# Gate products of the recurrence's branch in 1024-column halves, four of eight pieces by seven block products

## What is computed

```python
h = rmsnorm(x, g_pre_mix[l])
proj = h @ w_in[l]
q_in, ckv, k_rope, lru_x, lru_y, gate_mla, gate_lru = jnp.split(proj, IN_SPLIT_IDX, axis=-1)
o_mla = mla_attention(q_in, ckv, k_rope, positions, g_ckv[l], w_ukv[l]) @ w_o_mla[l]
...
o_lru = (hr * jax.nn.gelu(lru_y, approximate=True)) @ w_o_lru[l]
merged = jax.nn.sigmoid(gate_mla) * o_mla + jax.nn.sigmoid(gate_lru) * o_lru
x = x + rmsnorm(merged @ w_out[l], g_post_mix[l])
```

## Time and profile before

| | us |
|---|---|
| median of 3 runs | 1725.56 |
| lowest and highest | 1725.15, 1725.76 |
| profiled execution | 1725.27 |
| its span | 1723.5 |
| PE busy in the span | 1714.5 (99%) |
| DVE busy | 1211.6 (70%) |
| ACT busy | 949.1 (55%) |
| POOL busy | 216.4 (13%) |
| bytes moved | 355.29 MB, 206 GB/s on average |

### The profile page before, as it was taken

How to read it: one execution, slowest core, us unless ns; L and a number is a source line. 1 busy time by engine, 2 the same in 40 slices (tenths; PEclk the granted TensorE clock), 3 DMA queues, 4 the chain that set the end, 5 groups by cost and what they waited for, 6 DMA issues and landing times.

```text
span 1723.5 us, 25132 instructions
## 1 busy us (share of the span) xinstructions
PE 1714.5 (99%) x8920; PEld 1461.9 (85%) x8920; DVE 1211.6 (70%) x1517; ACT 949.1 (55%) x1203; POOL 216.4 (13%) x271
## 2 busy tenths in 40 slices
PE   9999999999999999999999999999999999999998
PEld 8888888888888888888888888888888888888886
DVE  7766665467788874446567687778877778977766
ACT  7656655443667763334446575555545556545553
POOL 0012212110345431100000001110001110000000
PEclk9999999999999999999999999999999999999999
DMA  9644458997556579976655455556755556775552
GB/s 342 201 133 156 153 197 266 270 300 212 180 176 183 182 247 268 259 226 227 216 176 188 147 197 194 192 176 212 248 195 176 181 181 207 247 242 181 194 218 99
DMA packets 228384, 355.29 MB, mean 206 GB/s; under 512 B 7264, under 2 KB 163552, under 8 KB 224736
## 3 DMA queue, kind: packets, MB, share of 16 engines
q1 hardware_dynamic: 215232, 322.72, 55.6%
q0 software_dynamic: 7168, 16.78, 5.3%
q10 hardware_dynamic: 5920, 14.94, 2.3%
HBM read 350.22 MB, written 20.97 MB: 215 GB/s over the span
## 4 chain that ended last, share of the span: by engine, by line
PE 89%; issue 5%; ACT 2%; DVE 2%; POOL 0%; ACTq 0%; DVEq 0%; POOLq 0%
PE ps L554 43%; PE ps L617 34%; PE ps L1033 4%; PE ps L570 3%; ACT wsp L1162 1%; DVE wsp L1697 1%; PE ps L829 1%; PE ps L757 1%; PE ps L679 1%; PE ps L668 0%; ACT wsp L1613 0%; PE ps L649 0%; PE ps L786 0%; PE ps L762 0%; POOL scr L2575 0%
## 5 line engine op out<-in xcount | busy, mean ns | idle before, releaser
L1697 DVE TENSOR_TENSOR wsp<-raw,wsp 128x2048 fp32r<-128x2048 f32 (+2 forms) x303 | 673.3, 2236 | 262.4 <-ACT wsp L1162 249.8
L1162 ACT ACTIVATE wsp<-raw 128x2048 fp32r<-128x2048 f32 (+2 forms) x288 | 529.4, 1852 | 203.2 <-PE ps L617 170.9
L554 PE MATMUL ps<-asp,wsp 128*128 128x512 f32 x3064 | 542.4, 339 | 0.0
L554 PEld LDWEIGHTS ps<-asp,wsp 128*128 128x128 f32 x3064 | 469.7, 188 | 70.3 <-DVE asp L2158 0.3
L617 PE MATMUL ps<-wsp,hsp 128*128 128x512 f32 x1908 | 437.2, 390 | 0.0
L617 PEld LDWEIGHTS ps<-wsp,hsp 128*128 128x128 f32 x1908 | 357.9, 188 | 74.1
L554 PE MATMUL ps<-hsp,wsp 128*128 128x512 f32 (+1 forms) x1936 | 349.7, 340 | 0.0
L554 PEld LDWEIGHTS ps<-hsp,wsp 128*128 128x128 f32 x1936 | 297.5, 188 | 42.9
L617 PE MATMUL ps<-wsp,asp 128*128 128x512 f32 x768 | 175.6, 389 | 0.0
L1173 ACT ACTIVATE cr<-ps 128x256 f32<-128x256 f32 x185 | 69.3, 380 | 190.1 <-PE ps L554 173.6
L617 PEld LDWEIGHTS ps<-wsp,asp 128*128 128x128 f32 x768 | 144.0, 188 | 29.8
(11 more groups left out here) (293 smaller groups left out, 1249.6 us busy)
## 6 DMA issues: line engine op xcount, KB each, us to landing
raw<-in_w_up SPq DMA_DIRECT2D x88, 1024.0 KB, 5.3
raw<-in_w_in SPq DMA_DIRECT2D x64, 1024.0 KB, 5.5
raw<-in_w_down SPq DMA_DIRECT2D x28, 1024.0 KB, 4.9
raw<-in_w_in SPq DMA_DIRECT2D x32, 768.0 KB, 4.4
dn_sums<-in_w_down POOLq DMA_DIRECT2D x64, 256.0 KB, 6.9
raw<-in_w_o_mla SPq DMA_DIRECT2D x16, 1024.0 KB, 10.7
raw<-in_w_o_lru SPq DMA_DIRECT2D x16, 1024.0 KB, 7.5
raw<-in_w_out SPq DMA_DIRECT2D x16, 1024.0 KB, 4.9
```

What stands on the lines that cost most here:

```text
L554: mm = pe.matmul(ps[:, bank, 0:w], lhs(part, k), x[:, 0:w], start=(f and part == 0), stop=(l and n == 1))
L1162: act.activation(wsp[:, p0 % SLOTS, 0, 0:n], raw[:, p0 % SLOTS, 0:n], ACT.Copy).then_inc(hi_done, 1)
L1697: dve.tensor_tensor(wsp[:, slot, 1, 0:n], raw[:, slot, 0:n], wsp[:, slot, 0, 0:n].bitcast(F32), ALU.subtract).then_inc(lo_done, 1)
```

## The change

`PH_OL` becomes four phases: a gate phase and an output phase for columns 0 to 1023, then both for columns 1024 to 2047 (`PH_GL`, `PH_OL`, lists of two).

A gate phase has 12 pieces after `GL_PLAN`: pairs 0, 2, 4 and 6 of row blocks as plain pieces of 2 x 1024 (eight block products each), pairs 1, 3, 5 and 7 as a first and a made piece (seven block products). The plain products go to banks 4 to 7, the shared ones to banks 0 to 3. An output phase has 8 pieces of 2 x 1024, in banks 0 to 3.

```diff
+GL_PLAN = [("plain", 0), ("plain", 2), ("first", 1), ("made", 1), ("first", 3), ("made", 3),
+           ("plain", 4), ("first", 5), ("made", 5), ("first", 7), ("made", 7), ("plain", 6)]
...
-PH_OL = Phase(PH_LRU, 4, [0, 0, 0, 2] * 2, crosses=False)
-PH_WO = Phase(PH_OL, 4, [0] * 4)
+PH_GL, PH_OL = [], []
+for _half in range(2):
+    PH_GL.append(Phase(PH_OL[-1] if PH_OL else PH_LRU, 1, [0] * 12, twice=GL_FIRST))
+    PH_OL.append(Phase(PH_GL[-1], 1, [0] * 8))
+PH_WO = Phase(PH_OL[-1], 4, [0] * 4)
```

The work of DVE in the two phases (`sums_rest`, `first_low` as before in the down products, now with the phase as argument):

```diff
+            for h in range(2):
+                for c in range(LEAD, len(GL_PLAN) + LEAD):
+                    if c in GL_FIRST:
+                        sums_rest(PH_GL[h], c)
+                        first_low(PH_GL[h], c)
+                    else:
+                        lo(PH_GL[h], 0, c)
+                    if h == 0 and c == LEAD:
                         y_lo(PH_LRU.trips - 1)
+                    if h == 1 and c == LEAD:
+                        ol_merge(0)
+                    if c == GL_MADE[-1] + 2:
+                        gl_products(h)
+                for c in range(LEAD, 8 + LEAD):
+                    lo(PH_OL[h], 0, c)
+                    if c == 3:
+                        gl_plain(h)
+                    if h == 1 and c == 6:
                         merged_lo(range(8))
...
+            ol_merge(1)
```

```diff
-            for cs in DN_SUMS:
-                weight_sums(0, cs, sums_done)
+            for batch in SUM_BATCHES[:3]:
+                weight_sums(*batch)
...
-            for cs in DN_SUMS:
-                weight_sums(1, cs, sums_done)
+            for batch in SUM_BATCHES[3:]:
+                weight_sums(*batch)
```

More of the change, by code:

```diff
@@ L833, in _ @@
             rounds(pe, PH_LRU, lru, first_apart=True)
-            enter(PH_OL, [0, 1, 2, 3])
             def turn_merged(ks):
@@ L844, in turn_merged, with form_mm @@
                     turn(a_tok, k, 4 + k // 2 % 4, (k % 2) * T, m_turned)
-            def o_lru(i):
-                last = isinstance(i, int) and i == PH_OL.trips - 1
+            def form_mm(bank, lhs, slot, block, first, last):
+                for t, (part, low) in enumerate(TERMS):
+                    mm = pe.matmul(ps[:, bank, :], lhs(low), wsp[:, slot, part, quarter(block)],
+                                   start=(first and t == 0), stop=(last and t == 2))
+                return mm
@@ L1028, in _ @@
                     rounds(pe, up, up_round)
[L1031 to L1035, removed]
                 def dn_half(h):
@@ L1375, in merged_hi, with made_high @@
                     act.activation(hsp[:, k, 0:T], ps[:, 4 + k // 2 % 4, (k % 2) * T:(k % 2 + 1) * T], ACT.Copy).then_inc(m_hi, 1)
[L1377 to L1389 removed]
+            def made_high(ph, c, at):
+                slot = (ph.p0 + c) % SLOTS
+                act.wait_ge(gemm_step, free_step(ph, c))
+                act.wait_ge(landed[slot], ph.landed(0, c))
+                act.wait_ge(sums_made, at + 1)
+                act.activation(wsp[:, slot, 0, :], raw[:, slot, :], ACT.Copy).then_inc(hi_done, 1)
@@ L1390, in o_lru @@
                         merged_hi(range(8))
-                    if last and c == 6:
-                        merged_hi(range(8, 12))
-            rounds(act, PH_OL, o_lru, first_apart=True, last_apart=True)
+            for h in range(2):
+                gl_half(h)
+                ol_half(h)
             def mem_high(ks):
@@ L2027, in _, with sums_rest @@
-            rounds(dve, PH_OL, o_lru, first_apart=True, last_apart=True)
+            def sums_rest(ph, c):
+                first, made = (raw[:, (ph.p0 + at) % SLOTS, :] for at in (c, c + 1))
+                for at in (c, c + 1):
+                    dve.wait_ge(landed[(ph.p0 + at) % SLOTS], ph.landed(0, at))
+                own.link(dve.tensor_tensor(made[:, 1024:1536], made[:, 0:512], first[:, 1024:1536], ALU.add))
+                dve.tensor_tensor(made[:, 1536:2048], made[:, 1024:1536], first[:, 1536:2048], ALU.add).then_inc(sums_made, 1)
```

378 lines of the change are left out of this document (260 added, 118 removed).

## The result

The changed kernel is slower. Ten runs have a median of 1731.61 us (1726.20 to 1735.81); ten runs of the kernel before have 1725.82 us (1725.15 to 1727.59). The ratio is 1.0028, 95% interval 1.0018 to 1.0037. It is one of the longer ones: the ten runs spread over 9.6 us, and the three shortest (1726.20, 1726.52 and 1728.51 us) have a mean granted clock of 0.999, the other seven, from 1730.38 us on, 0.997 or 0.998.

A forecast was written before the change was run, and what follows sets the result against it. The prediction took the stage to be bound by PE alone, at its matmul rate. 1725.27 - 5.44 (matmuls removed) + 1.28 (waiting) = 1721.1; with the runs' median 0.29 above that execution, 1721.4 us, range 1720.0 to 1724.2.

The forecast's parts named there:

- The 24 matmuls: Gate, both halves: 12 fewer matmuls of 512 columns each, at 0.2267 us, saving 5.44 us.
- The start of the first half: First gate half, third to sixth piece: PE waits for DVE 1.28 us in all, 0.3 before the fourth piece.
- Rival B: First gate half's start: POOL's multiplication comes after DVE's three operations; 3.0 us of waiting, 1723.1 us; chance 0.16.
- The second gate half has no wait: Second gate half: DVE has a large lead at the first pair, so PE has no new wait.
- The sums of `h`, the gate's sums and `PH_WO`: Before, in and after the recurrence's branch: added or moved sums and output-bank order costed at nothing.
- The loads of the first gate half: First gate half, made pieces: loads land in 4.3 to 7.3 us, losing 0 to 1.0 us, taken as 0.
- rival C: Gate, first half: made pieces' loads land in 7 to 9 us; 1722.1 to 1724.1 us; chance 0.17.
- The new form has no dearer matmul: Gate pairs: a 512-column matmul costs 0.2267 us in the seven-product form, as in the plain one.
- changes between plain pieces: Gate, 40 pieces where there were 32: a change of piece costs PE nothing when the piece is ready.
- the banks of the products: Start of output phases: PE asks 5.44 us after the last made piece, four DVE operations take 2.8 us; costed at nothing.
- rival D: Gate, both halves: made pieces' loads land in up to 13.2 us, losing 11.3 us; 1731.4 us; chance 0.06.

The follow-up runs named there:

- e11: Changed kernel with 3 of POOL's 16 sums between the output phases' load bursts, 13 behind them, and the third plain piece ahead of the second pair: 1720.76 us.
- e1: Changed kernel with POOL's 16 down-product sums begun near 756 us instead of near 626 us: 1722.70 us, ratio 0.9989 to the kernel before.
- e6: Changed kernel with POOL's sums late, bank copy and four DVE operations ahead of the splits, third plain piece ahead of the second pair: 1725.65 us.
- e2: Changed kernel with ACT's copy of the first bank and DVE's four bank operations queued ahead of the output pieces' splits: 1727.13 us, ratio 1.0004.
- e9: The kernel of e6 run once more, unchanged, for a trace of a longer run: 1726.47 us.
- e10: Changed kernel with the third plain piece moved between the third and fourth pair, POOL's sums left from 626 us on: 1726.48 us, ratio 1.0005.

## Why the prediction was wrong

It gave 1721.4 us, a range of 1720.0 to 1724.2, and 0.06 for slower. Its terms, one by one:

**Right.** The 24 matmuls, 5.44 us (e11 shows all of it). The start of the first half: 1.28 us of waiting forecast; in e1, where no load disturbs it, that half loses 1.32 us, of which 0.42 also stand in the second half, where nobody waits, so 0.9 is the start. Its mechanism is shown by e6, where a plain piece ahead of the second pair takes it away. Rival B is refuted: POOL's last `y_mult` ran in DVE's first gap, as its timeline in the changed kernel shows:

```profile
624.74 1.04 POOL L2733 TENSOR_TENSOR scr<-scr 128x256 f32<-128x256 f32 x1 [0.70 <-DVE scr L2151]
```
The second gate half has no wait. The sums of `h`, the gate's sums and `PH_WO` cost nothing, as forecast.

**Mis-sized.** The loads of the first gate half: a landing of 4.3 to 7.3 us and 0 to 1.0 us lost, taken as 0. Between 624 and 645 us the made pieces landed in 6.6 us and the plain one in 7.8 (in e1 3.4 and 5.0), and 3.00 - 1.32 = 1.7 us were lost. That is rival C's mechanism, at the made pieces and at the plain one, and its sign is there, an addition of DVE's that waits for a load of sums:

```profile
641.94 0.69 DVE L2175 TENSOR_TENSOR raw<-raw 128x512 f32<-128x512 f32 x1 [1.80 <-DMA raw<-sums]
```

"The new form has no dearer matmul": the 42 matmuls of two pairs take 734.26 - 724.53 = 9.73 us in the second half, where nobody waits, against the 9.52 of the earlier trace rows. That is the 0.42 us of each half; changes between plain pieces cost nothing, as forecast. Why the pairs of the gate are dearer than those of the down products isn't shown.

**The step that failed** is "the banks of the products: PE asks for them 24 matmuls (5.44 us) after its last made piece, four DVE operations take 2.8 us", costed at nothing. It counted the four operations and not what stands ahead of them in the queues: ACT's copy behind two splits, each of which waits for a load. That the loads could be late was priced for the made pieces alone, where they are used at once, and rival D, too, put its loss there. For the 1 MB pieces of the output product, where the burst is four loads in 13 us, no landing time was asked for. They cost 5.46 us at the first output phase and 1.49 at the second. The 13.3 us at which they landed is just the size of the 13.2 of the earlier trace rows that rival D used for the made pieces, and the argument against it (half the size, the memory columns moved away) held for the made pieces only. Behind that wait the 2.87 us of the clock weren't in any rival.

Together: 1.72 more in the first gate half (3.00 against 1.28), 5.46, 2.87, 1.49, 0.42, and 0.27 of small ones make 12.2 us, the distance from 1721.1 to the profiled 1733.3. All but the 0.42 and the small ones are gone in e1.

## What to carry to other kernels

When pieces get smaller or cheaper, slots come free faster: add up the bytes asked for in the fastest stretch and what else uses the DMA engines then, for every piece behind it, not only for the new ones. For each operation that a later product needs, list what stands ahead of it on its engine and what that waits for; an operation behind the split of a piece that is still to land inherits the landing time. Background transfers belong between the bursts, and their end needs room before the next use of the queue that issued them, or it shows in some runs and not in others.

## What the hardware showed

**POOL's accumulating copies took more of the DMA engines than their bytes.** From 645 to 658 us q0 took 40.0% of the engines' time for 0.81 MB, 0.156 MB/us of the time it held, q1 50.9% for 2.32 MB, 0.351; with the sums away q1 moved 4.75 MB in 98.5%, 0.371. The size of the packets is not the reason. In the kernel before, from 656 to 662 us, both queues move packets of about 2 KB:

```profile
q0 software_dynamic: 429, 0.78, 72.7%
q1 hardware_dynamic: 396, 0.78, 36.0%
```

The same bytes hold the engines twice as long on POOL's queue (0.179 against 0.361 MB/us). These are accumulating copies, asked for from 652.36 on. POOL's plain copies are not dear: from 640 to 645 us in the kernel before q0 moves 0.52 MB in 26.5%, 0.39 MB/us. No run moved one kind without the other, so how much of the loss each kind made is open.

The Trainium skill ("DMA: Bandwidth & Descriptors", "Queues, rings and completion order") says that each DMA engine takes its queues in turn, packet by packet, where a packet is a group of descriptors. The traces agree in part: 429 packets to 396 above, and 276 to 318 in the changed kernel from 652 to 658 us, where q1's are twice as large (0.50 and 1.26 MB), look like turns by packet and not by bytes. The 131 to 55 from 649 to 652 us, with a load of q1 still to land, do not. No row shows whether the profile's packets are those of the page.

**The clock after idling.** An idle time of 5.3 us took the granted clock to 0.50 and cost 2.87 us more. An idle time of 2.6 us (e2) was followed by 0.57 from 664.6 to 668 us and cost 664.64 to 709.61, 44.97 - 43.52 = 1.45 us; the 3.3 us of e9 by 0.73 from 1024 to 1030 us. After 1.3 us (changed kernel, second half) and after 1.0 and 1.7 us (e10) it stayed at 1.00, and the matmuls behind took 0.1 to 0.2 us more. In these rows the two long waits cost about half as much again, which no list of waits shows.

**Landing times.** Loads of `w_o_lru` of 1 MB landed in 6.2 us (median of four) with the sums away, in 10.6 beside them in a thinned burst, in 13.3 beside them in the full one.
